# Decoder step with mixture of experts on one core: a seventh ring slot, four expert chunks in reused buffers, feature-major memory keys and earlier table loads

## What is computed

```python
kv = rmsnorm(mem_prompt, mem_norm[i]) @ w_mem_kv[i]        # keys, values: (256, 1024) each, for each layer
for i in range(2):
    h = rmsnorm(x, norm_mix[i]); z = h @ w_in[i]           # 4096 columns in layer 0, 7168 in layer 1
    mix = conv or retention of z; xa = cross_attn(q_x, mem_k[i], mem_v[i])
    x = x + concat(mix, xa) @ w_out[i]
    x = x + hier_moe(rmsnorm(x, norm_ffn[i]), ...)
# hier_moe, per token:
g = argmax(h @ w_group); top 2 of the 8 experts of group g; weights from the two softmaxes
act = silu(h @ w_gate) * (h @ w_up) * weight; y = act @ w_down     # 32 experts, 1024 -> 2 x 256 -> 1024
y = rmsnorm(x, final_norm)
```

## Time and profile before

| | before |
|---|---|
| median of three runs | 1340.07 us |
| profiled execution | 1339.78 us, span 1337.9 us, mean TensorE clock 0.955 |
| moved | 364.59 MB, mean 273 GB/s |
| experts, layer 0 / layer 1 (first gate/up to the end of the last combine) | 358.1 to 594.6 us / 1096.0 to 1318.0 us |
| largest shares of the chain that ended last | waits for in_gu 24%, L621 21%, L429 12%, L330 8% |

### The profile page before, as it was taken

One profiled execution on the slowest core, in us unless ns is written; L12 is line 12 of the kernel. 1 busy time (PEld: TensorE's weight loads), 2 busy tenths in 40 slices (PEclk: granted clock), 3 DMA queues, 4 the chain that ended last, 5 costly groups with the idle time before them and its releaser, 6 DMA issues.

```text
span 1337.9 us, 13595 instructions
## 1 busy us (share of the span) xinstructions
PE 1204.8 (90%) x5884; PEld 693.8 (52%) x5884; DVE 355.2 (27%) x868; ACT 153.9 (12%) x340; POOL 11.2 (1%) x22
## 2 busy tenths in 40 slices
PE   6999998998998989869999999996999889888785
PEld 3467776776333434236655555563677743332233
DVE  3222213004021304223234342422300233222224
ACT  2000002002110101010201010110200021000001
POOL 0000000000000000000000000000000000000000
PEclk9999999998999999889999999998999869989998
DMA  9743338731599999994216565557954419999991
GB/s 397 302 159 126 126 128 321 313 126 63 216 430 428 421 428 428 427 427 188 79 63 238 218 227 229 216 240 303 425 188 169 176 34 430 427 428 428 428 426 75
DMA packets 27263, 364.59 MB, mean 273 GB/s; under 512 B 3152, under 2 KB 3168, under 8 KB 5056
## 3 DMA queue, kind: packets, MB, share of 16 engines
q1 hardware_dynamic: 23904, 338.99, 62.1%
q10 hardware_dynamic: 1696, 18.88, 3.4%
q0 software_dynamic: 1600, 5.81, 1.1%
HBM read 339.34 MB, written 24.32 MB: 272 GB/s over the span
## 4 chain that ended last, share of the span: by engine, by line
PE 69%; DMA 26%; DVE 2%; ACT 2%; issue 1%; POOL 0%; SPq 0%; DVEq 0%; POOLq 0%; ACTq 0%
DMA ring<-in_gu 24%; PE bank L621 21%; PE bank L429 12%; PE bank L330 8%; PE bank L486 4%; PE bank L706 4%; PE bank L476 2%; PE bank L517 2%; PE bank L316 1%; PE bank L677 1%; PE bank L442 1%; PE bank L385 1%; PE bank L787 1%; PE bank L408 1%; PE bank L768 1%
## 5 line engine op out<-in xcount | busy, mean ns | idle before, releaser
L621 PE MATMUL bank<-hT,ring 128*128 128x288 f32 x1152 | 285.7, 409 | 4.0 <-DVE hT L1077 3.3
L621 PEld LDWEIGHTS bank<-hT,ring 128*128 128x128 f32 x1152 | 218.8, 191 | 73.7 <-issue 13.9
L486 PE MATMUL bank<-ring,arena 128*32 128x512 f32 x1024 | 132.7, 656 | 55.0 <-DMA ring<-in_gu 53.3
L429 PE MATMUL bank<-arena,ring 128*128 128x288 f32 x640 | 155.7, 406 | 1.8 <-DVEq L1141 1.8
L429 PEld LDWEIGHTS bank<-arena,ring 128*128 128x128 f32 x640 | 121.4, 190 | 35.6 <-issue 2.2
L330 PE MATMUL bank<-ring,arena 128*128 128x512 f32 x256 | 111.2, 594 | 3.1 <-DVE arena L1077 3.1
L486 PEld LDWEIGHTS bank<-ring,arena 128*32 128x32 f32 x1024 | 32.5, 115 | 146.8 <-DMA ring<-in_gu 80.2
L476 PE MATMUL bank<-arena 128*128 128x512 f32 (+1 forms) x192 | 102.0, 659 | 2.4 <-DVE arena L1207 1.7
L330 PEld LDWEIGHTS bank<-ring,arena 128*128 128x128 f32 x256 | 48.2, 190 | 63.4 <-issue 61.9
L517 PE MATMUL bank<-arena 128*128 128x288 f32 x256 | 71.4, 427 | 2.1 <-issue 1.7
L476 PEld LDWEIGHTS bank<-arena 128*128 128x128 f32 (+1 forms) x192 | 32.9, 198 | 73.9 <-issue 72.4
(11 more groups left out here) (206 smaller groups left out, 806.1 us busy)
## 6 DMA issues: line engine op xcount, KB each, us to landing
ring<-in_gu SPq DMA_DIRECT2D x64, 2048.0 KB, 24.9
ring<-in_dn SPq DMA_DIRECT2D x32, 2048.0 KB, 17.4
ring<-in_rin SPq DMA_DIRECT2D x14, 2048.0 KB, 13.4
ring<-in_wkv SPq DMA_DIRECT2D x8, 2048.0 KB, 17.4
ring<-in_cin SPq DMA_DIRECT2D x8, 2048.0 KB, 8.7
ring<-in_kc SPq DMA_DIRECT2D x8, 2048.0 KB, 8.6
ring<-in_vc SPq DMA_DIRECT2D x8, 2048.0 KB, 14.0
ring<-in_st SPq DMA_DIRECT2D x8, 2048.0 KB, 14.9
```

The costliest lines, as they stand in the source:

```text
L429: mm = pe.matmul(bank[1 + o % 4][:, 0:T], w[:, k, :], cat[:, k, :], start=(k == 0), stop=(k == kt - 1))
L486: mm = pe.matmul(bank[2][32 * e:32 * e + 32, :], xt[:, k, 32 * e:32 * e + 32], wv[:, e, kk, :], start=(k == 0), stop=(k == KD - 1), skip_g ...
L621: mm = pe.matmul(outs[o], w[:, o, k, :], src[:, k, :], start=(k == 0), stop=(k == KD - 1))
```

## The change

- R becomes 7; the overflow code keeps using 6 slots (SPILL).
- Four gate/up chunks leave the ring (EXTRA). Each is loaded in two halves into buffers that no one uses during the experts: gu(0,1,1) and gu(1,1,2) over qx and qm (behind the routing tables), gu(1,1,1) over KT and V, gu(1,1,3) over the first part of hT and HM1. SP issues them at their place in the list, after waits for the last users of those buffers (`load_beside`). The ring is counted over the other chunks (RING).
- The keys are computed feature-major: a 128 x 128 block of the key weights is loaded, the 256 memory tokens move. The result is KT itself; the transposes, Ktok and keys1 go, the output is laid out as KT and reordered on the host. TensorE waits for four key copies (done early) and for the value copies before the input projection.
- One-element activations (`idle`) of Sqrt ahead of each squares pass, of Exp ahead of the attention's softmax and after the root of ffn0 and ffn1.
- TensorE, ScalarE and VectorE load the number of passes before the last pack in place of after it; the jump stays.
- The norm scratch (nrm) and tanh scratch (th) move inside the arena, which shrinks; qm is cleared again on VectorE after the mix1 norm; VectorE no longer waits for the key store there; POOL's descriptor scratch is cut to 2048 bytes a partition.

```diff
-R = 6
+R = 7
+SPILL = 6
...
-AT = {name: n for n, name in enumerate(SEQ)}
-SPILL_AT = {len(SEQ_A + pack_sequence(0)) - 1: 0, len(SEQ) - 1: 1}
+EXTRA = {("gu", (0, 1, 1)): 0, ("gu", (1, 1, 1)): 1, ("gu", (1, 1, 2)): 2, ("gu", (1, 1, 3)): 3}
+RING = [name for name in SEQ if name not in EXTRA]
+AT = {name: n for n, name in enumerate(RING)}
+SPILL_AT = {("dn", (l, PACKS - 1, 1)): l for l in range(2)}
...
+        def beside(name):
+
+            half = SLOT // 2
+            o = (PHO + ROUTE, KTO, PHO + ROUTE)
+            kind = EXTRA[name]
+            if kind == 3:
+                return hT_[:, 0:half], ar(HM1, half)
+            return ar(o[kind], half), ar(o[kind] + half, half)
...
-            for n, name in enumerate(SEQ):
+            def load_beside(name):
+
+                l = name[1][0]
+                kind = EXTRA[name]
+                if kind < 2:
+                    sp.wait_ge(S("dec_pv"), 4 * l + 4)
+                if kind == 1:
+                    sp.wait_ge(S("keys_stored1"), 16)
+                    sp.wait_ge(S("values_stored1"), 16)
+                if kind in (0, 2):
+                    sp.wait_ge(S("conv_stored"), 32)
+                    sp.wait_ge(S("normed"), NORM_DONE[f"ffn{l}"])
+                if kind == 3:
+                    sp.wait_ge(S("ret_stored"), 16 * H)
+                    sp.wait_ge(S("h_turned"), 12)
+                src, dst = source(name), beside(name)
+                for q in range(2):
+                    sp.dma_start(dst[q], src[:, q * (SLOT // 2):(q + 1) * (SLOT // 2)]).then_inc(S(f"beside{kind}"), 16)
+
+            for name in SEQ:
+                if name in EXTRA:
+                    load_beside(name)
+                    continue
+                n = AT[name]
                 if n >= R:
-                    wait_used(sp, SEQ[n - R])
+                    wait_used(sp, RING[n - R])
...
+                if c < 2:
+                    for o in range(2):
+                        f = (2 * mb + o) * P
+                        for k in range(KD):
+                            if i == 0 and j == 0 and o == 0:
+                                pe.wait_ge(S("normed"), k + 1)
+                            mm = pe.matmul(bank[KV_BANKS[i][j]][:, o * NM:(o + 1) * NM], w[:, k, f:f + P],
+                                           src[:, k, :], start=(k == 0), stop=(k == KD - 1), skip_group_check=True)
+                    mm.then_inc(S("kv_sum"), 1)
+                    return
...
+                    if i == PACKS - 1:
+                        pe.wait_ge(S(f"npass{L}"), 1)
+                        more = pe.value_load(npass[0:1, L:L + 1], min_val=0, max_val=PASSES - 1)
...
-                    if L == 0 and i in KEYS_IN:
-                        pe.wait_ge(S("gt_out"), i)
-                        turn_keys(1, KEYS_IN[i])
-                        pe.wait_ge(S("kt_out_a"), 2 + KEYS_IN[i][1] + 1)
...
-                pe.wait_ge(S(f"npass{L}"), 1)
-                more = pe.value_load(npass[0:1, L:L + 1], min_val=0, max_val=PASSES - 1)
                 with pe.If(more > 0):
...
-            pe.wait_ge(S("ktok_out"), 4)
-            turn_keys(0, range(4))
-
-            pe.wait_ge(S("kt_out_a"), 2)
-            pe.wait_ge(S("kt_out_d"), 2)
+            pe.wait_ge(S("kt_out"), 4)
             pe.wait_ge(S("v_out"), 4)
...
+                act.activation(idle, C("eps")[0:1, :], ACT.Sqrt)
                 for k in range(KD):
                     ready(k)
...
+                if name in ("ffn0", "ffn1"):
+                    act.activation(idle, C("eps")[0:1, :], ACT.Exp)
...
                 act.wait_ge(S("normed"), NORM_DONE[f"mix{i}"])
+                act.activation(idle, C("eps")[0:1, :], ACT.Exp)
...
-            dve.wait_ge(S("keys_stored1"), 16)
             norm("mix1", xT, ((hT, "mix1"),), T)
 
+            V_(dve.memset(qm_, 0.0))
...
-    nc = bacc.Bacc("TRN2", target_bir_lowering=False, num_devices=1)
+    nc = bacc.Bacc("TRN2", target_bir_lowering=False, num_devices=1, dynamic_dma_scratch_size=2048)
```

More of the change, by code:

```diff
@@ L122, in build @@
         small = sb("small", 96)
-        arena = sb("arena", 21568)
+        arena = sb("arena", 20992)
         bank = [ctx.enter_context(nc.psum_tensor(f"bank{i}", [P, 512], F32)) for i in range(8)]
@@ L177, in build @@
         STd = ar(dec + 2048, TD)
-        th = [ar(MSO + 288 * i, T) for i in range(2)]
+        th = [ar(SQO + 1184 + 288 * i, T) for i in range(2)]
         bn6, mv, gv = small[:, 36:48], small[:, 48:52], small[:, 52:56]
-        nrm = ar(MSO, 576)
+        idle = small[0:1, 62:63]
+        nrm = ar(PHO + 2752, 576)
         ms, rstd = nrm[:, 0:288], nrm[:, 288:576]
@@ L205, in build @@
         npass = small[:, 60:62].bitcast(I32)
-        assert ro[0] <= QMO
+        ROUTE = 1408
+        assert ro[0] <= PHO + ROUTE and PHO + ROUTE + SLOT <= 20992
         htok = [ar(CATO + 1024 * i, 1024) for i in range(3)]
@@ L289, in spill @@
                             sp.wait_ge(S(f"spill_dve{L}"), p * (STEP_DVE * PACKS) + i * STEP_DVE + SPILL_DVE["began"])
-                            for j in range(R):
+                            for j in range(SPILL):
                                 src = a["gu"][bass.ds(i * 4 + (L * 4 * PACKS + j), 1)] if j < 4 else \
@@ L303, in _ @@
                     sp.dma_start(xT, a["xT"]).then_inc(S("x_in"), 16)
-                if n in SPILL_AT:
-                    spill(SPILL_AT[n])
+                if name in SPILL_AT:
+                    spill(SPILL_AT[name])
         @block.tensor
@@ L326, in memory_kv @@
                 w = v3(landed(pe, (f"kv{i}", c)), KD)
+                if c < 2:
[8 more added lines that the diff above has]
+                    return
                 for k in range(KD):
-                    if i == 0 and j == 0:
-                        pe.wait_ge(S("normed"), k + 1)
                     mm = pe.matmul(bank[KV_BANKS[i][j]][:, :], src[:, k, mb * P:(mb + 1) * P], w[:, k, :],
@@ L478, in picked, with halves, gate_up_landed @@
                 return mm
+            def halves(w):
+                return w[:, 0:SLOT // 2], w[:, SLOT // 2:SLOT]
+            def gate_up_landed(L, i, c):
+                name = ("gu", (L, i, c))
+                if name in EXTRA:
+                    pe.wait_ge(S(f"beside{EXTRA[name]}"), 32)
+                    return beside(name)
+                return halves(landed(pe, name))
             def gate_up_chunk(c, w, xt):
-                wv = w.rearrange("p (e k n) -> p e k n", e=PK, k=2)
+                wv = [h.rearrange("p (e k n) -> p e k n", e=PK // 2, k=2) for h in w]
                 for kk in range(2):
@@ L592, in experts @@
                             for c in range(4):
-                                pe.wait_ge(S(f"spill_landed{L}"), it * (16 * R) + 16 * R)
-                                mm = gate_up_chunk(c, slot(c), xgT_x)
+                                pe.wait_ge(S(f"spill_landed{L}"), it * (16 * SPILL) + 16 * SPILL)
+                                mm = gate_up_chunk(c, halves(slot(c)), xgT_x)
                             mm.then_inc(S(f"spill_pe{L}"), 1)
@@ L954, in experts @@
                 for i in range(PACKS):
+                    if i == PACKS - 1:
+                        act.wait_ge(S(f"npass{L}"), 1)
+                        more = act.value_load(npass[0:1, L:L + 1], min_val=0, max_val=PASSES - 1)
                     act.wait_ge(S("gu_sum"), 4 * PACKS * L + 4 * i + 4)
@@ L1255, in experts @@
                 for i in range(PACKS):
+                    if i == PACKS - 1:
+                        dve.wait_ge(S(f"npass{L}"), 1)
+                        more = dve.value_load(npass[0:1, L:L + 1], min_val=0, max_val=PASSES - 1)
                     dve.wait_ge(S("tanh"), PACKS * L + i + 1)
@@ L1273, in experts @@
                 add_pack(PACKS - 1)
-                more = dve.value_load(npass[0:1, L:L + 1], min_val=0, max_val=PASSES - 1)
                 with dve.If(more > 0):
```

57 lines of the change are left out of this document (14 added, 43 removed).

## The result

| | before | after |
|---|---|---|
| median | 1340.12 us (1339.09 to 1340.31) | 1289.29 us (1284.29 to 1289.88, 4 runs) |
| profiled execution | 1339.78 us, span 1337.9, clock 0.955 | 1284.29 us, span 1282.5, clock 0.974 |

The mechanism forecast for the experts came as described. A term of 2.0 us, the two stretches behind the experts, was really 13.

A forecast was written before the change was run, and what follows sets the result against it. Weight transfers were taken to bound the two expert stages and TensorE the rest. The terms summed to -37.3 us from the profiled 1339.78, giving 1302.5, or a median of 1302.8 us; range 1294 to 1313.

The forecast's parts named there:

- Register loads and jump: Idle stretches before the sums of squares behind the experts: loading the pass count earlier gains 1.0 us in each layer.
- Theory R: Idle time behind the experts: the register load was all of it, 6.2 us in layer 0 and 3.4 in layer 1.
- Rival C: Idle time behind the experts: the register load was most of it, 9.6 us go instead of 2.0, 1295.2 us; chance 0.13.
- Experts, layer 1: Second expert stage: ten chunks instead of six are there at its start, 17.0 us gained after a 2.7 us DMA hole.
- Rival A: Expert stages: displaced chunks bring nothing because SP reaches them too late, only the seventh slot counts, 1319.8 us; chance 0.07.
- Experts, layer 0: First expert stage: two more chunks are moved in the DMA's idle time ahead of it, 9.8 us gained, no hole.
- Rival B: Expert stages: TensorE becomes the bound in places or a second hole comes, 3 to 6 us less gained; chance 0.13.
- Key transposes: Before the input product: TensorE no longer turns the keys and waits only for the last value copy, 1.6 us gained.
- Rival D: Key products: they become bound by their weight loads, +48.6 us, 1351 us in all; chance 0.02.
- Attention 1's stall: Decoder scores of attention 1: the fourth key chunk arrives earlier with seven slots, 3.8 us gained.
- Attention 0: Between decoder scores and values of attention 0: a table load leaves the path, 2.4 us gained by comparison with attention 1.
- Route 1: Routing ahead of the layer 1 experts: a table load no longer holds back VectorE's weights chain, 0.7 us gained.

The follow-up runs named there:

- again: The changed kernel run and traced once more with no edit: 1292.7 us, ratio 0.9648.

## Why the prediction missed, step by step

**Register loads and jump: the step that failed.** The prediction took 1.0 us of each idle stretch because "the jump stays", and so its time. The jump stayed and its time went: 8.1 and 5.1 us with the sums. Its reading that a good part of the stretch was a fetch was right; that the fetch would stay with the jump was wrong. Theory R's part was 0.3 to 0.9 us, even less than the 1.0 taken; the rest belonged to where the compiled code lay relative to blocks of 256 instructions. The feature-major keys double some matmuls and drop the transposes, 192 instructions more ahead of both jumps, which moved the jumps from places 184 and 206 to 120 and 142. The Trainium skill (Runtime: NRT & Kernel Launch, Instruction fetch mechanics), which the prediction cited, names the condition, a taken branch whose target isn't in the window held; the traces agree: each of the nine standstills ends 2.4 to 2.8 us after a packet of code. I read it as a property of the jump and not of its place. The row that could have told was in the trace of before, the packet at 598.11 in the idle stretch; I didn't look at that queue in a narrow window. Each stretch also carried a second cost: behind the standstill the 16 products ran at 0.72 and 0.74 of the full clock, 5.70 and 5.53 us, and straight behind busy work at 1.00, 4.04 us. The windows of the two sums before, and of the first one after:
```profile
600.83:606.53 5.70, 5.70 (x16) 3.94 (x16) 0.00 (x0) 0.00 (x0) 0.00 (x0) 0.72 1.00 423
1321.41:1326.94 5.53, 5.53 (x16) 3.89 (x16) 0.00 (x0) 0.00 (x0) 0.00 (x0) 0.74 0.01 3
```
```profile
578.31:582.35 4.04, 4.04 (x17) 2.85 (x15) 0.62 (x2) 1.05 (x3) 0.00 (x0) 1.00 1.01 424
```
Rival C named the size of this case and the warmer clock, but gave the wrong cause.

**Experts, layer 1: right.** 17.0 forecast, 16.7 (again) and 18.7 (after, its tail 2.2 us shorter at the full clock). The eight traces with these homes lie between 203.3 and 205.7 us, so the 18.7 is the upper end. The displaced chunks were in before the stage. Hole: forecast 2.7, measured 2.8. Rival A holds only with six slots.

**Experts, layer 0: right as a sum.** 9.8 forecast, 11.5 and 12.5 in the table; by the middle traces of either program (236.0 and 225.8) 10.2. But the split, 4.9 for the slot and 4.9 for the home, didn't hold: the slot brought most of it. No second hole came: before has 395 GB/s from 445 to 455 us, and after is not below 419 in any 5 us from 430 to 465. Rival B falls with it.

**Key transposes: right.** The input product starts 0.83 us after the memory product instead of 2.44, 1.6 forecast. Rival D fell: the first four key products take 27.86 us, against 27.70, so the weight loads of 190 ns stayed hidden.

**Attention 1's stall: right.** 3.7 us in after and 5.1 in again, where 1.5 of it is TensorE's busy time (312.4 us in place of 313.9); 3.8 forecast; the last wait, which is now one and not two, is 7.13 us:
```profile
904.73 3.38 PE L383 MATMUL bank<-ring,arena 128*32 128x256 f32 x32 [7.13 <-DMA ring<-in_kc]
```

**Attention 0: the sum is right by luck.** 2.4 us came, of which 1.0 is the table and 1.4 the clock. Comparing the two attentions mixed the two. The drain that the prediction weighed beside it doesn't show on this path: the run without early tables prices the load below its own 1.28 us.

**Route 1: too small.** 0.8 forecast with the norm's share; 2.8 more came in after, of it 2.5 by a gather product at a better clock (7.97 against 10.45 us), which again didn't repeat; there it was 1.1 more.

**The range.** It made no allowance for a clock that differs between executions of one program by several us. Its ends don't follow from the terms either: with the best bound of every term (1.28 at each of the two ffn norms) the sum gives 1288, not 1291, so the measured 1289.3 lay inside the bounds and outside the range; and the worst leaves out the 3 us named under covers.

## What to carry to other kernels

When a stretch is idle with nothing released, look at the instruction queue's packets in a narrow window before pricing it: a packet in it says that the time belongs to where the code lies, and any edit ahead of it can remove it or bring it back. So a gain or loss of several us behind a jump should be tested with a few instructions that do nothing before it is credited to an edit. Space in a ring pays only if the order of issue reaches it in time: here three homes were worth 13 to 15 us in the second stage with a seventh slot, and nothing without it.

## What the runs showed of the hardware

A taken jump of some 300 instructions on TensorE cost 2.2 to 6.2 us beside the expert weights' traffic (423 to 432 GB/s) and 2.5 to 3.4 us on a quiet DMA, or nothing, by its place in the code; work goes on 2.4 to 2.8 us after the packet of code. The products behind such a standstill lost another 1.5 to 2.0 us per 16 at a granted clock of 0.68 to 0.74. The value load itself cost 0.3 to 0.9 us. An instruction that only counts a semaphore took about 0.15 us of TensorE's queue: its first product starts at 10.74 us behind 64 of them, at 13.18 behind 80 and at 18.06 behind 112.
